# A transfer of filter weights and two sine layers, reshaped from 64 to 128 partitions, in a two-block transformer kernel

## The reference, cut to what matters

```python
h = jnp.sin(freq_1 * (z @ w_f1 + b_f1))      # z: 256 x 33, w_f1: 33 x 64
h = jnp.sin(freq_2 * (h @ w_f2 + b_f2))      # w_f2: 64 x 64
k = (h @ w_f3).reshape(L, HY_ORDER, 2, HY_WIDTH)   # w_f3: 64 x 2048
...
k = k * decay[:, None, None, :]
```

## Time and profile before

| | us |
|---|---|
| median of 3 runs (lowest, highest) | 791.05 (790.72, 791.93) |
| the profiled execution | 791.88 |
| its span, first to last instruction | 790.1 |
| TensorE matmul busy in the span | 732.2 (93%) |
| VectorE, ScalarE busy | 476.9 (60%), 328.1 (42%) |
| mean granted TensorE clock | 0.97 |
| bytes moved | 190.00 MB, 240 GB/s over the span |

### The profile page before, as it was taken

One profiled execution on the slowest core, in us unless ns is written; L12 is line 12 of the kernel. 1 busy time (PEld: TensorE's weight loads), 2 busy tenths in 40 slices (PEclk: granted clock), 3 DMA queues, 4 the chain that ended last, 5 costly groups with the idle time before them and its releaser, 6 DMA issues.

```text
span 790.1 us, 11044 instructions
## 1 busy us (share of the span) xinstructions
PE 732.2 (93%) x4596; PEld 546.3 (69%) x4596; DVE 476.9 (60%) x886; ACT 328.1 (42%) x488; POOL 17.9 (2%) x15
## 2 busy tenths in 40 slices
PE   7999999999999999977899798679999989999998
PEld 7988886778778885544345254247899958687786
DVE  6898858756657647322252131138686689896763
ACT  6565437646364415110111010037665543366630
POOL 0000000000000000000000000001100003000000
PEclk9999999999999999996789899899999999999999
DMA  9765443243368689899999999995553643453311
GB/s 318 240 227 167 159 159 114 97 132 135 106 246 309 245 346 397 317 362 421 421 421 397 421 421 421 416 396 191 167 198 104 232 166 108 128 190 107 108 53 54
DMA packets 63156, 190.00 MB, mean 240 GB/s; under 512 B 7481, under 2 KB 11835, under 8 KB 51132
## 3 DMA queue, kind: packets, MB, share of 16 engines
q1 hardware_dynamic: 61326, 184.44, 62.8%
q10 hardware_dynamic: 1774, 4.79, 1.8%
HBM read 188.16 MB, written 1.05 MB: 239 GB/s over the span
## 4 chain that ended last, share of the span: by engine, by line
PE 73%; DMA 16%; DVE 6%; ACT 3%; issue 1%; POOL 0%; SPq 0%; ACTq 0%; DVEq 0%
PE pb L518 69%; DMA WHo<-in_w_exp_up 8%; DMA raw<-in_w_exp_up 6%; PE pb L527 4%; DMA WHo<-in_w_exp_down 2%; DVE rawo L1803 1%; ACT arena L1312 1%; ACT WH L1284 1%; DMA c<-in_cst 1%; DVE arenao L1837 0%; DVE arena L1857 0%; POOL small L2730 0%; SPq L2777 0%; DVE arena L2120 0%; DVE HDl L1837 0%
## 5 line engine op out<-in xcount | busy, mean ns | idle before, releaser
L1284 ACT ACTIVATE WH<-raw 128x2048 fp32r<-128x2048 f32 (+5 forms) x80 | 145.4, 1825 | 85.1 <-PE pb L518 76.8
L1803 DVE TENSOR_TENSOR rawo<-raw,WH 128x2048 fp32r<-128x2048 f32 (+5 forms) x80 | 172.5, 2174 | 3.9 <-ACT WH L1284 3.7
L518 PE MATMUL pb<-WH,HTh 128*128 128x512 f32 (+2 forms) x352 | 142.0, 403 | 3.0 <-ACT arena L1312 1.4
L518 PE MATMUL pb<-rawo,HTh 128*128 128x512 f32 (+2 forms) x352 | 135.1, 384 | 0.0
L518 PE MATMUL pb<-WH,HTl 128*128 128x512 f32 (+2 forms) x352 | 135.0, 384 | 0.0
L518 PEld LDWEIGHTS pb<-WH,HTh 128*128 128x128 f32 x352 | 66.2, 188 | 20.4 <-issue 6.6
L518 PEld LDWEIGHTS pb<-rawo,HTh 128*128 128x128 f32 x352 | 66.2, 188 | 13.1
L518 PEld LDWEIGHTS pb<-WH,HTl 128*128 128x128 f32 x352 | 66.4, 189 | 11.5 <-issue 0.7
L518 PE MATMUL pb<-WH,arenao 128*128 128x512 f32 x224 | 69.6, 392 | 2.4 <-ACT arena L1312 1.2
L518 PE MATMUL pb<-arena 128*32 128x256 f32 (+6 forms) x252 | 58.7, 432 | 3.4 <-ACT arena L1708 2.6
L2358 DVE TENSOR_TENSOR rt_<-rt_,pb 128x256 f32<-128x256 f32 x8 | 3.4, 422 | 92.6 <-ACT rt_ L1571 92.6
(11 more groups left out here) (370 smaller groups left out, 1266.1 us busy)
## 6 DMA issues: line engine op xcount, KB each, us to landing
raw<-in_w_in SPq DMA_DIRECT2D x46, 1024.0 KB, 5.1
raw<-in_w_exp_up SPq DMA_DIRECT2D x18, 1024.0 KB, 21.8
arena<-in_w_exp_gate SPq DMA_DIRECT2D x13, 1024.0 KB, 20.6
arena<-in_w_exp_down SPq DMA_DIRECT2D x12, 1024.0 KB, 16.4
WHo<-in_w_exp_down SPq DMA_DIRECT2D x9, 1024.0 KB, 24.1
raw<-in_w_out SPq DMA_DIRECT2D x8, 1024.0 KB, 5.3
raw<-in_w_exp_gate SPq DMA_DIRECT2D x8, 1024.0 KB, 17.4
WHo<-in_w_exp_up SPq DMA_DIRECT2D x8, 1024.0 KB, 22.7
```

The lines of the kernel that those rows point to most:

```text
L518: return e.matmul(o, l, r, start=start, stop=stop, skip_group_check=True)
L1284: e.activation(h_, r_, ACT.Copy).then_inc(hi.sem, hi.mark(k))
L1803: e.tensor_tensor(l_, r_, h_.bitcast(F32), ALU.subtract).then_inc(lo.sem, lo.mark(k))
```

## The change

`FW` is now 128 partitions of 1024 columns: partitions 0 to 63 hold the first 1024 columns of `w_f3`, partitions 64 to 127 the last 1024. The source is written as a three-dimensional view, halves x 64 rows x 1024 columns. So that both halves of the partitions have the sine values to multiply with, `w_f1` and `w_f2` are each loaded twice side by side, the two layers give 128 rows (the 64 values twice), and biases and frequencies are put into both halves of `col2` by two small matmuls in place of one transposition. `kernel_rows` picks the upper or lower 64 partitions by n. `f1` and `f2` move into the arena's columns 16192 to 16448, which the narrower `FW` gives free.

```diff
-        col2 = sm(4, parts=64)
+        col2 = sm(4)
...
-        FW = arena[0:64, 15168:17216]
+        FW = arena[:, 15168:16192]
...
-        f1 = arena[0:33, 18752:18816]
-        f2 = arena[0:64, 18816:18880]
-        FH = arena[0:64, 14656:15168].rearrange("p (a l) -> p a l", a=2)
+        f1 = arena[0:33, 16192:16320]
+        f2 = arena[0:64, 16320:16448]
+        FH = arena[:, 14656:15168].rearrange("p (a l) -> p a l", a=2)
...
-                mul(o[0:64, 0:256], wgt, src).then_inc(mm.sem, mm.mark(("fh", n)))
+                mul(o[:, 0:256], wgt, src).then_inc(mm.sem, mm.mark(("fh", n)))
...
-                mul(o[:, :], FH[:, 1, (n // 4) * 128:(n // 4) * 128 + 128],
-                    FW[:, (n % 4) * 512:(n % 4) * 512 + 512]).then_inc(mm.sem, mm.mark(("kf", n)))
+                upper = slice(64 * (n % 4 // 2), 64 * (n % 4 // 2) + 64)
+                mul(o[:, :], FH[upper, 1, (n // 4) * 128:(n // 4) * 128 + 128],
+                    FW[upper, (n % 2) * 512:(n % 2) * 512 + 512]).then_inc(mm.sem, mm.mark(("kf", n)))
...
-                    turn(o[0:64, 0:4], rows2[:, :])
+                    for half in (0, 64):
+                        mul(o[half:half + 64, 0:4], rows2[:, :], ident[0:4, 0:4])
...
-                    for dst, src in ((FW, flat("w_f3_2")), (f1, flat("w_f1_2")), (f2, flat("w_f2_2")),
+                    halves = lambda a: a.rearrange("k (h n) -> h k n", h=2)
+                    for dst, src in ((FW, halves(flat("w_f3_2"))), (f1[:, 0:64], flat("w_f1_2")),
+                                     (f1[:, 64:128], flat("w_f1_2")), (f2[:, 0:64], flat("w_f2_2")),
+                                     (f2[:, 64:128], flat("w_f2_2")),
...
-                e.tensor_scalar(FH[:, 0, :], pb(("fh", n))[0:64, 0:256], col2[:, 2 * n:2 * n + 1],
+                e.tensor_scalar(FH[:, 0, :], pb(("fh", n))[:, 0:256], col2[:, 2 * n:2 * n + 1],
```

More of the change, by code:

```diff
@@ L1057, in tensor @@
                     ac.wait_ge(e, ("fh", 0))
-                    filter_layer(1, f2[:, :], FH[:, 1, :])
+                    filter_layer(1, f2[:, :], FH[0:64, 1, :])
                 if q == 3:
@@ L2380, in vector @@
                     mm.wait_ge(e, "col2")
-                    e.tensor_copy(col2, pb("col2")[0:64, 0:4])
+                    e.tensor_copy(col2, pb("col2")[:, 0:4])
                     e.memset(pair, 1.0)
```

## The result

The changed kernel takes 797.15 us (median of 5 runs, 795.21 to 798.99), the kernel before 790.72 (5 runs, 789.01 to 791.93): ratio 1.0081 with an interval of 1.0057 to 1.0105, so 0.8% slower, 6.4 us. Its profiled execution took 798.99 us with a span of 797.2.

A forecast was written before the change was run, and what follows sets the result against it. Bound until about 523 us by bytes on DMA engines, then by TensorE. Two engines' 14.3 us less 3.1 replaced gave +11.2: 803.1 us from the profiled 791.88, about 802.3 from the median; own range 798 to 806.5, stated 794 to 811.

The forecast's parts named there:

- The bound: Until about 523 us, the expert tiles: bytes on DMA engines set the time; behind that, TensorE, left unchanged.
- How many engines: The new w_f3 transfer: outermost counts 128 and 2 put it on 2 DMA engines, with 940 packets in ScalarE's queue.
- What two engines cost: The w_f3 load beside the expert tiles: 14.3 us on each engine, less 3.1 spent before, net +11.2 us.
- lower end: The w_f3 load on two engines at 26.3 GB/s each: 10.0 us, net +6.9 us.
- rival C: Two engines, but overlapped packets and TensorE's gaps make the lag smaller: +3 us, 794 us; chance 0.08.
- The replaced term: The old w_f3 load, which goes: 1.2 us for its bytes plus 1.9 us for crowding, 3.1 us.
- upper end: The w_f3 load on two engines at a crowded stretch's rate, 14.1 GB/s each: 18.6 us, net +15.5 us.
- The lag reaches the end: From w_f3 to the last expert tile: the two engines cannot catch up, so the whole lag, +11.2 us, stays.
- The wait for d_filt: TensorE before sine layer 0: w_f3 lands near 379 us, up tiles by 380 too, so nothing extra.
- Rival B: End of step 0: two engines, and ScalarE held at its issues until 361 us; perhaps 5 us more, 807; chance 0.15.
- Rival A: The w_f3 transfer: the destination's 128 decides, sixteen engines, 1.9 us (up to 2.7) come back, 789.1; chance 0.12.
- The rest: Doubled w_f1 and w_f2, VectorE's sine layers and one more transposition: 0.06, 2.2 off the path and under 0.3 us.

The follow-up runs named there:

- e10: The kernel before without the transfer of w_f3: 787.18 us against 791.13, ratio 0.9942.
- e3: The changed kernel with its two-engine transfer of w_f3 issued by SyncE, amid the expert tiles, on its own semaphore: 799.1 us against 790.56 for the kernel before.
- e5: The changed kernel with w_f3 issued by ScalarE at the end of step 1 instead of step 0, on its own semaphore: 799.17 us against 790.83 for the kernel before.
- e12: The changed kernel with w_f3 issued last of ScalarE's step 0 transfers and waited for only before the filter rows: 798.14 us against 791.13 for the kernel before.
- e7: The kernel before with w_f3's source read as 2 x 32 rows, every other row (two engines, 8 KB packets, 64 partitions): 803.31 us against 790.83.
- e11: The kernel before with w_f3 read by every other row in two transfers of 1024 columns (two engines, 64 packets of 4 KB each): 799.35 us against 791.13.
- e2: The kernel before with ScalarE kept busy about 20 us by twenty copies after step 0's transfers, no transfer changed: 793.22 us against 790.56.
- e8: Against the kernel before: w_f3 in 128 partitions, halves of each row in neighbouring partitions, sixteen engines, only sine layer 1 doubled: 787.76 us against 790.83.
- e1: The changed kernel with w_f3 loaded by two transfers of 64 rows x 1024 columns, each on sixteen engines: 790.26 us against 790.56 for the kernel before.

## Why the prediction was right, and where its size was off

**The bound.** Right. The loss lies ahead of the last expert tile. Behind it come 266.7 us, 267.0 before, and 265 to 268.5 in the experiments whose chain ends on that tile.

**How many engines.** Right, and this decided the sign. 940, 754, 752 and 758 packets are those that two, four, two and eight engines give by the count of reports. The Trainium skill ("DMA: Bandwidth & Descriptors", Why a DMA increments its semaphore by 16 and not by 1) has the rule that the count is the largest up to 16 that divides the slowest dimension of both sides; by that rule the trace agrees, with 940.

**What two engines cost.** The mechanism was right, the term was too large: +11.2 was forecast, +6.4 measured, just below the forecast's lower end of +6.9. 797.15 us lies outside the forecast's own range, 798 to 806.5, and inside the stated one, 794 to 811, which was drawn wider for rival C (+3). The failed choice is "I take the middle, 14.3". The whole load costs 6.4 + 4.0 (e10, the cost of the load that it replaces) = 10.4 us, or 262,144 bytes at 25 GB/s: close to the lower end, 10.0 us at 26.3 GB/s. The same transfer issued otherwise costs 12.5 (e3), 12.3 (e5) and 11.0 us (e12), 21 to 24 GB/s, and its own packets in the changed kernel take 11.3 us on each engine. So the lower end is near, but a little too cheap. A stretch at 225 GB/s was no row for this transfer. That rate belongs to a load that sixteen engines write into 64 partitions at once, and in the changed kernel the rate was 402 in the same 4 us and never under 345 while the share was full. Nor is 225 the rate of w_f3 alone: it counts the packets of the tiles beside it, which go to 128 partitions. The replaced term was sized at 3.1 and measured 4.0 (2.8 to 6.4, so 3.1 isn't excluded). By the medians, of the 4.8 us between forecast and result 3.9 lie in the lag and 0.9 in what it replaces. With 64 partitions the upper end, 18.6, was the nearer one in e7: 12.5 + 4.0 = 16.5 us. e11, in the same partitions with 4 KB packets, gives 8.2 + 4.0 = 12.2. The partitions alone therefore don't choose the end.

**The lag reaches the end.** Right. 7.4 us at the last piece (two single executions), 6.4 at the kernel's end (medians). With another engine's issue (e3) or a later one (e5) the last piece ends at 530.86 and 530.13, so the lag stays there too. The shares of the profile don't prove it by their size. 0.87, 0.99 and 0.89 in three stretches of 20 us miss 2.8 + 0.4 + 2.4 = 5.6 us of a full 1.01, and 14 of 16 engines standing for 6.4 us would be 5.6; but 0.6 us were missing before as well (0.98 from 400 to 420 us), and e2 has the first of these falls with no uneven transfer. That the two figures of 5.6 agree is luck.

**The wait for d_filt.** "The up tiles come by 380 us too" was wrong: step 2's Silu came at 371.86, and TensorE then stood for 8.51 us until the layer at 383.19. "Nothing extra" was right for the path: e12 takes this wait away and gains nothing that can be measured. What holds is the prediction's own "inside the same 11", with 6.4 us in place of 11. The layer's time, about 384 us forecast, came out by luck in part: it was worked out from 0.29 us for a packet of 4 KB, which took 0.177, and the last of w_f3's packets began at 381.6 us all the same.

**Rival B.** It was given 0.15 and its mechanism happened: issues of 24.6 us, Silu 18.5 us late. Its 5 us didn't. In e3, e5 and e12 ScalarE has no hold, and they lose 8.5, 8.3 and 7.0 us. That TensorE catches up while it waits for tiles that come no sooner fits this, but no run shows it by itself. e2's 2.7 us show that such a hold isn't free where the tiles are on time. The row on which B was built was misread: SyncE's 10.1 us at 336.1 us are two issues of 1.6 us together with a wait of 8.6 us for TensorE between them, and say little of how many packets a queue takes. What shows that a queue can hold its engine are the changed kernel, e3 and e11.

**Rival C.** It was given 0.08 at +3 us. The change lost more, 6.4 us with an interval of 4.5 to 8.3, and no run shows C's reasons at work; but the measured size lies between C and the forecast's lower end.

**Rival A.** It was false of this transfer, since two engines carry it. Its gain exists: 1.9 (up to 2.7) us were expected from taking the crowding away, and e8 measured 2.5 (1.3 to 3.8). e1, sixteen engines in two pieces, doesn't have it (ratio 0.9999); one transfer of this layout on sixteen engines was not measured, and e8 is the nearest to it.

**The rest.** VectorE's steps at 128x256 take 0.29 us where 64x256 took 0.28 (VectorE's timeline in the changed kernel):

```profile
385.00 0.29 DVE L1880 TENSOR_SCALAR arena<-arena 128x256 f32<-128x256 f32 x1
```

With e1 that makes the doubling free within 1.1 us.

## What to carry to other kernels

Count the reports in a queue's packets to see how many engines a transfer has, and write its view so that the outermost count of both sides is a multiple of 16; a view with the halves ahead puts all on two. Where a load runs beside a stream that keeps all DMA engines busy, the bytes on its most loaded engine at that engine's share of the full rate are the least that it costs: 10.0 us for two engines here, where 10.4 to 16.5 were measured, and 5.0 us for four, where it was 10.0. That cost stays until the stream ends. An issue that takes long, and what waits for it, is dramatic in a timeline and may cost nothing; take it away before you believe it. And before you read a long row of several issues as a held queue, look how long each of them took.

## What the runs showed of the hardware

- Eight engines instead of sixteen cost nothing into 64 partitions (ratio 1.0000 [0.9985, 1.0016]), four cost 0.8%, two 1.7% with packets of 8 KB and 1.1% with packets of 4 KB (e11). With the 4.0 us of e10, the most loaded engine's bytes went at 65,536 / 4.0 = 16 GB/s, 131,072 / 10.0 = 13 GB/s, 262,144 / 16.5 = 16 GB/s and, in e11, 262,144 / 12.2 = 21 GB/s; in 128 partitions at 21 to 25. The 4.0 us are themselves known only to 2.8 to 6.4.
- Two transfers into 64 partitions each, which together fill 128, still pull a full stream down to 272 GB/s; one into 128 neighbouring partitions leaves it at 415.
- A transfer with 64 packets of 4 KB on one engine holds the issuing engine at the issues behind it, not at its own: 13.79 + 1.60 + 9.16 us in the changed kernel, 11.62 us for SyncE's next fetch in e3, and 0.62 us for the transfer itself when it is ScalarE's last (e5, e12). SyncE's tiles are held later all the same: one issue of 11.5 to 11.9 us there, 4.2 before.
